# Seven half-width products for eight in the gate and up projections of two feed-forward layers

## The chip, the cores and the metric

The kernel runs on one core of a Trainium2 chip. The metric is the device time of one execution in microseconds (us), as the median of several runs.

## What is computed

Two transformer blocks run one after the other on one sequence of 512 tokens with a model width of 1024, in float32. The change touches their two feed-forward layers (D_FF is 2816):

```python
u = rms_norm(h, norm_ffn_g[l])
g, up = jnp.split(u @ w_gate_up[l], 2, axis=-1)
h = h + (jax.nn.silu(g) * up) @ w_down[l]
...
h = rmsnorm(x, g_ffn_pre[l])
gu = h @ w_ffn_in[l]
f = (jax.nn.silu(gu[..., :D_FF_2]) * gu[..., D_FF_2:]) @ w_ffn_out[l]
x = x + rmsnorm(f, g_ffn_post[l])
```

Around them stand attention, an mLSTM, gates and projections, which the change leaves as they are.

## The kernel before

**Data.** Activations are held transposed: 1024 features are 8 tiles of 128 partitions by 512 tokens (`hT`, float32). A float32 product is made of three matmuls in a rounded format, since each factor is split into a high part (the value rounded) and a low part (the rest): high times high, high times low, low times high (`split_mm`, L527 to L529). The normalised input is `u_hi` and `u_lo`, each 8 tiles; the products of gate and up are `a_hi` and `a_lo`, 22 tiles each (`FT` is 22).

**Weights.** All weights of the program are one stream of tiles of 128 x 1024 (512 KB), in the order of use. Tile t goes through a ring of three slots (`R` is 3). SyncE loads it into `w_raw` (the loop at L417) once the low part of tile t-3 is made. ScalarE rounds it into `w_hi` (`feed`, L1229, recorded at L1234) once TensorE has done with tile t-3 (semaphore `w_used`). GpSimd then makes `w_lo = w_raw - w_hi` (`low_part`, L440, recorded at L443), for nearly all tiles. TensorE waits for `lo_ready`.

**Up stages.** In `ffn1` and `ffn2` (44 tiles each) the tiles alternate: one of gate weights, one of up weights. Each is a unit of 24 matmuls of 512 columns into one PSUM bank (`tile_unit`, L531): 8 feature tiles by three. Six units, three pairs, are a turn of the loop (`tiles_loop`, L625). VectorE's part of a pair is `pair` in `ffn_dve` (L2335): the gate is scaled by the norm's factor (L2337), ScalarE takes its sigmoid (L1657), two multiplications of SBUF tiles follow (L2342, L2343), then the up product out of PSUM (L2345), and the high and low part of the result (L2348, L2349). The norm's factor comes late, so that it is multiplied in behind the matmuls (`root`, L1261; the matmul at L684 or L1139).

**Down stages.** `down` (L642) reads `a_hi` and `a_lo`. Its first unit waits until 20 of 22 tiles are split, its last for all of them.

Every engine has its own queue in program order. On VectorE, `step` lets each instruction wait until the one before it is done.

## Time and profile before

| | us |
|---|---|
| median of 3 runs (1701.81 to 1701.96) | 1701.86 |
| span of the profiled execution | 1699.9 |
| PE busy in that span | 1690.9 (99%) |
| DVE busy | 883.4 (52%) |
| ACT busy | 656.4 (39%) |
| POOL busy | 682.4 (40%) |

PE is TensorE, PEld its loading of stationary tiles, DVE VectorE, ACT ScalarE, POOL GpSimd, SP SyncE. The profiled execution's span is 2.0 us shorter than the median of the runs.
### The profile page before, as it was taken

Reading aid. Unit: us, or ns where it says so; the run is one execution under the profiler, and the core shown is the slowest. Engines: PE = TensorE matmul, PEld = TensorE weight load, DVE = VectorE, ACT = ScalarE, POOL = GpSimd, SP = SyncE. Lnnn points to the kernel's source line nnn. Section 1 sums busy time; section 2 is a strip of 40 time slices with the busy share of each in tenths; the row PEclk is TensorE's granted clock in tenths of the full one; section 3 lists DMA queues with packets and bytes.
Section 4 is the critical chain, followed back from the end, with each engine's and each line's share of the span. In section 5 each row is a group of like instructions: output and inputs, shape, how many; then the busy total and the mean of one; then the engine's idle time right before and its main releaser. Section 6 shows DMA issues by size and latency. Waiting matters only on the chain.

```text
span 1699.9 us, 23574 instructions
## 1 busy us (share of the span) xinstructions
PE 1690.9 (99%) x8081; PEld 1359.4 (80%) x8085; DVE 883.4 (52%) x1406; ACT 656.4 (39%) x1091; POOL 682.4 (40%) x308
## 2 busy tenths in 40 slices
PE   9999999999999999999999999999999999999998
PEld 7888767788888888888788766678888988888887
DVE  6644875564655551217497676642233775555013
ACT  7333544433222223327424576452223522222122
POOL 2444322344544444445343102544444344444443
PEclk9999999999999999999999999999999999999999
DMA  5345321223333223334322111122233232332332
GB/s 202 115 152 152 102 63 51 75 87 124 99 99 98 90 97 99 99 98 138 128 88 87 50 38 51 51 74 90 96 99 99 88 99 92 94 98 99 99 97 65
DMA packets 47635, 162.29 MB, mean 95 GB/s; under 512 B 5724, under 2 KB 7900, under 8 KB 47304
## 3 DMA queue, kind: packets, MB, share of 16 engines
q1 hardware_dynamic: 43440, 150.70, 28.1%
q10 hardware_dynamic: 4120, 10.59, 1.9%
q8 instruction: 46, 0.75, 0.2%
q14 instruction: 29, 0.24, 0.0%
HBM read 156.91 MB, written 4.76 MB: 95 GB/s over the span
## 4 chain that ended last, share of the span: by engine, by line
PE 52%; issue 32%; POOL 12%; ACT 1%; DVE 1%; DMA 1%; POOLq 0%; SPq 0%; ACTq 0%; DVEq 0%
PE ps L527 14%; PE ps L529 14%; PE ps L528 14%; POOL w_lo L443 12%; PE ps L1153 1%; PE ps L1152 1%; PE ps L1151 1%; PE ps L708 1%; PE ps L726 1%; PE ps L752 1%; PE ps L1052 1%; PE ps L1011 1%; PE ps L1033 1%; PE ps L980 1%; DMA hT<-xT 0%
## 5 line engine op out<-in xcount | busy, mean ns | idle before, releaser
L443 POOL TENSOR_TENSOR w_lo<-w_raw,w_hi 128x1024 fp32r<-128x1024 f32 x260 | 643.2, 2476 | 892.8 <-ACT w_hi L1234 866.1
L527 PE MATMUL ps<-u_hi,w_hi 128*128 128x512 f32 x1336 | 540.0, 404 | 0.2 <-ACTq L1824 0.2
L529 PE MATMUL ps<-u_hi,w_lo 128*128 128x512 f32 x1336 | 521.7, 390 | 0.0
L528 PE MATMUL ps<-u_lo,w_hi 128*128 128x512 f32 x1336 | 521.3, 390 | 0.0
L1234 ACT ACTIVATE w_hi<-w_raw 128x1024 fp32r<-128x1024 f32 x271 | 285.5, 1055 | 391.9 <-PE ps L529 326.4
L527 PEld LDWEIGHTS ps<-u_hi,w_hi 128*128 128x128 f32 x1336 | 251.2, 188 | 58.5 <-issue 8.6
L529 PEld LDWEIGHTS ps<-u_hi,w_lo 128*128 128x128 f32 x1336 | 250.9, 188 | 53.0
L528 PEld LDWEIGHTS ps<-u_lo,w_hi 128*128 128x128 f32 x1336 | 251.4, 188 | 51.1 <-issue 1.4
L1657 ACT ACTIVATE tmp<-tmp 128x512 f32<-128x512 f32 x44 | 27.8, 632 | 213.2 <-DVEq L2339 213.2
L2349 DVE TENSOR_TENSOR a_lo<-tmp,a_hi 128x512 f32 (+1 forms) x44 | 104.2, 2368 | 4.7
L527 PE MATMUL ps<-a_hi,w_hi 128*128 (+1 forms) x264 | 103.0, 390 | 0.0
L529 PE MATMUL ps<-a_hi,w_lo 128*128 (+1 forms) x264 | 102.8, 390 | 0.0
L528 PE MATMUL ps<-a_lo,w_hi 128*128 (+1 forms) x264 | 102.8, 390 | 0.0
L2345 DVE TENSOR_TENSOR tmp<-ps,tmp 128x512 f32<-128x512 f32 x44 | 30.4, 692 | 91.5 <-PE ps L529 91.2
L477 POOL TENSOR_TENSOR masked_bias<-bias,pick 128x128 f32<-128x128 f32 (+3 forms) x32 | 25.5, 824 | 104.5 <-PE ps L1052 103.7
L2337 DVE TENSOR_TENSOR tmp<-ps,tmp 128x512 f32<-128x512 f32 x44 | 30.4, 692 | 57.5 <-PE ps L529 43.9
L2306 DVE TENSOR_TENSOR tmp<-ps,tmp 128x512 f32<-128x512 f32 x16 | 11.1, 692 | 91.1 <-PE ps L529 90.0
L527 PEld LDWEIGHTS ps<-a_hi,w_hi 128*128 128x128 f32 x264 | 49.6, 188 | 10.4
L529 PEld LDWEIGHTS ps<-a_hi,w_lo 128*128 128x128 f32 x264 | 49.6, 188 | 10.3
L528 PEld LDWEIGHTS ps<-a_lo,w_hi 128*128 128x128 f32 x264 | 49.6, 188 | 10.1
L527 PE MATMUL ps<-m_hi,w_hi 128*128 128x512 f32 (+1 forms) x152 | 54.4, 358 | 0.0
L528 PE MATMUL ps<-m_lo,w_hi 128*128 128x512 f32 (+1 forms) x152 | 54.1, 356 | 0.0
(408 smaller groups left out, 2485.8 us busy)
## 6 DMA issues: line engine op xcount, KB each, us to landing
w_raw<-stream SPq DMA_DIRECT2D x277, 512.0 KB, 3.5
g_rep<-g_one ACTq DMA_DIRECT2D x1, 2560.0 KB, 13.7
spread<-m_rows ACTq DMA_DIRECT2D x4, 512.0 KB, 4.2
tmp<-tmp ACTq DMA_DIRECT2D x32, 64.0 KB, 2.7
bias<-g_rep ACTq DMA_DIRECT2D x1, 2048.0 KB, 9.7
outT<-hT SPq DMA_DIRECT2D x13, 128.0 KB, 2.0
hT<-xT SPq DMA_DIRECT2D x3, 512.0 KB, 7.0
mem_in<-memT ACTq DMA_DIRECT2D x1, 1024.0 KB, 4.7
```

Source lines behind the costliest of these rows:

```text
L443: pool.tensor_tensor(w_lo[:, slot], w_raw[:, slot], w_hi[:, slot].bitcast(F32), ALU.subtract)\
L477: pool.tensor_tensor(masked_bias[s % 4][:, 0:n], bias[:, h, T - n:T], pick[:, MOFF[t]:MOFF[t] + n], ALU.add).then_inc(named("dsa_bias"), 1)
L527: pe.matmul(out, wh, xh, start=start, stop=False)
L528: pe.matmul(out, wh, xl, start=False, stop=False)
L529: return pe.matmul(out, wl, xh, start=False, stop=stop)
L708: m = pe.matmul(ps[:, 2 + e, 0:keys[t]], head_q(h, t), head_k(h, keys[t]), start=True, stop=not extra(t))
L726: m = pe.matmul(ps[p0:p1, b, t * P:t * P + P], values(h, kb), prT[e][:, kb * P:kb * P + P], start=kb == 0, stop=kb == nb - 1)
L1234: act.activation(w_hi[:, slot], w_raw[:, slot], ACT.Copy).then_inc(hi_ready, 1)
L1657: act.activation(tmp[0][:, :], tmp[1][:, :], ACT.Sigmoid).then_inc(named(name + "_e"), 1)
L2337: step(dve.tensor_tensor(tmp[1][:, :], ps[:, banks[0], :], tmp[3][:, :], ALU.mult))
L2345: step(dve.tensor_tensor(tmp[4][:, :], ps[:, banks[1], :], tmp[2][:, :], ALU.mult))
L2349: step(dve.tensor_tensor(a_lo[:, bass.ds(k, 1)], a, a_hi[:, bass.ds(k, 1)].bitcast(F32), ALU.subtract))
```

## The change

Of every three pairs of the two up stages, two are computed by a scheme of Strassen's kind: a 2 x 2 product of blocks with seven block products in place of eight. The blocks are halves of the 1024 features, halves of the 512 tokens, and the gate and the up tile. A block product is 12 matmuls of 256 columns (`half_product`), a pair 84 of them, where it was 48 of 512 columns. The third pair stays as it was. `ffn1` has 6 such turns after 6 plain units, `ffn2` has 5 after 12, and 2 plain units close each stage.

Sums of weights are new (`weight_sums`, `s_raw`), and their split (`s_hi` on ScalarE, `s_lo` on VectorE in `sums_low`); sums of activations and their split (`t_sums`, `t_low`), four tiles once per stage; and sums of products out of PSUM (`copy` on ScalarE, `late_sums`, `late_up`, `fast_gate` on VectorE). The gate's sigmoid is written to PSUM bank 3 for these pairs, and `fast_up` multiplies there. The products of gate and up are kept as `a_raw` and split behind the last turn: the high part on ScalarE (`split`), the low part on VectorE. `down` waits for two more tiles before each of its units. SyncE waits for the weight sums before two of the six loads of a turn. The load of `mem_in` moves to the last turn of `ffn1`. `plain_gate`, `plain_mid` and `plain_up` hold the four multiplications of the old `pair` (one, two and one). Several semaphores are merged.

```diff
...
+                    for j in range(2 * R):
+                        t = u + R + j
+                        low, summed = i * (2 * R) + (t - R + 1), of_fast(name, "sum", i * 2 + (j // 2 + 1))
+                        if j in (0, 2):
+                            sp.wait_ge(*summed)
+                        sp.wait_ge(lo_ready, low)
+                        sp.dma_start(w_raw[:, t % R], stream[bass.ds(i * (2 * R) + t, 1)].rearrange("a p n -> (a p) n"))\
+                          .then_inc(landed[t % R], 16)
...
+            def half_product(out, w_h, w_l, x_h, x_l, start, stop):
+                for k in range(HK):
+                    pe.matmul(out, w_h(k), x_h(k), start=start and k == 0, stop=False, skip_group_check=True)
+                    pe.matmul(out, w_h(k), x_l(k), start=False, stop=False, skip_group_check=True)
+                    m = pe.matmul(out, w_l(k), x_h(k), start=False, stop=stop and k == HK - 1, skip_group_check=True)
+                return m
...
+                pe.wait_ge(lo_ready, t + 1)
+                acquire(x)
+                half_product(ps[:, x, L], *natural(a, 0), *of_u(0, L), True, False)
+                pe.wait_ge(*of_fast(name, "s_lo", i * 2 + (e + 1)))
+                half_product(ps[:, x, H], *summed(1), *of_t(2), False, True).then_inc(prod, 1)
+                acquire(y)
+                half_product(ps[:, y, L], *summed(0), *of_t(1), True, False)
+                pe.wait_ge(lo_ready, t + 2)
+                half_product(ps[:, y, H], *natural(b, 0), *of_t(0), False, True).then_inc(prod, 1)
+                pe.wait_ge(*of_fast(name, "copied", i * 2 + (e + 1)))
+                half_product(ps[:, x, L], *natural(a, 1), *of_u(1, L), False, True).then_inc(w_used, 1)
+                half_product(ps[:, x, H], *natural(b, 1), *of_t(3), False, True).then_inc(w_used, 1)
+                pe.wait_ge(*of_fast(name, "z", i * 2 + (e + 2)))
+                half_product(ps[:, y, H], *summed(2), *of_u(1, H), False, True).then_inc(named("fast_s_used"), 1)
...
+                    summed(i, pair)
+                    act.wait_ge(*of_fast(name, "s_used", i * 2 + (pair % 3 + 2 * (pair // 3) + 1)))
+                    act.activation(s_hi[pair % 3][:, :, :], s_raw[:, :, :], ACT.Copy).then_inc(named("raw_hi"), 1)
...
+                def copy(i, e):
+                    act.wait_ge(*of_fast(name, "prod", i * 4 + (2 * e + 1)))
+                    act.wait_ge(*of_fast(name, "z", i * 2 + (e + 1)))
+                    act.activation(first_two[:, :], ps[:, ffn2_banks(e)[0], :], ACT.Copy)\
...
+                def turn(i, last):
+                    feed_at(i, 2)
+                    copy(i, 0)
+                    sums_hi(i, 1)
+                    feed_at(i, 3)
+                    feed_at(i, 4)
+                    gate(ps[:, E_BANK, :])
+                    copy(i, 1)
+                    feed_at(i, 5)
+                    feed_at(i, 6)
+                    gate(ps[:, E_BANK, :])
...
+                        sums_hi(i, 3)
+                        feed_at(i, 7)
+                        plain_gate()
+                first(FIRST[name], plain_gate, t_tile, sums_hi)
...
+            def one_turn(u, gate, t_tile, sums_hi):
+                feed_after(u)
+                t_tile(0)
+                t_tile(1)
+                root("n_ffn", T)
+                feed_after(u + 1)
+                sigmoids()
+                gate()
+                feed_after(u + 2)
+                t_tile(2)
+                t_tile(3)
+                feed_after(u + 3)
+                gate()
+                feed_after(u + 4)
+                sums_hi(0, 0)
+                feed_after(u + 5)
+                gate()
...
+                    if k >= 2:
+                        dve.wait_ge(*of_fast(name, "t_hi", k - 1))
+                    t1, t2, t3, t4 = [t_raw[k % 2][:, n] for n in range(4)]
+                    step(dve.tensor_scalar(b11, hT[:, k, L], col, None, ALU.mult))
+                    step(dve.scalar_tensor_tensor(out=t1, in0=hT[:, k, H], scalar=col, in1=b11,
+                                                  op0=ALU.mult, op1=ALU.subtract))
+                    step(dve.scalar_tensor_tensor(out=t2, in0=hT[:, HK + k, H], scalar=late, in1=t1,
+                                                  op0=ALU.mult, op1=ALU.subtract))
+                    step(dve.tensor_tensor(t3, t2, b11, ALU.subtract))
+                    step(dve.scalar_tensor_tensor(out=t4, in0=hT[:, HK + k, L], scalar=late, in1=t2,
+                                                  op0=ALU.mult, op1=ALU.subtract))
+                    dve.sem_inc(named("fast_sum"), 1)
...
+                def t_low(k):
+                    dve.wait_ge(*of_fast(name, "t_hi", k + 1))
+                    step(dve.tensor_tensor(t_lo[:, k], t_raw[k % 2][:, :, :], t_hi[:, k].bitcast(F32), ALU.subtract))
+                    dve.sem_inc(named("raw_lo"), 1)
...
+                def weight_sums(i, pair):
+                    c = u + 2 * pair
+                    a, b = c % R, (c + 1) % R
+                    for t in (c, c + 1):
+                        dve.wait_ge(landed[t % R], i * 32 + (16 * (t // R) + 16))
+                    step(dve.tensor_tensor(s_raw[:, 1], w_raw[:, a, 0:T], w_raw[:, b, 0:T], ALU.subtract))
+                    step(dve.tensor_tensor(w_raw[:, b, 0:T], w_raw[:, b, 0:T], w_raw[:, b, T:2 * T], ALU.add))
+                    step(dve.tensor_tensor(s_raw[:, 0], w_raw[:, b, 0:T], w_raw[:, a, 0:T], ALU.subtract))
+                    step(dve.tensor_tensor(s_raw[:, 2], w_raw[:, a, T:2 * T], s_raw[:, 0], ALU.subtract))
+                    dve.sem_inc(named("fast_sum"), 1)
+                def sums_low(i, pair):
+                    dve.wait_ge(*of_fast(name, "s_hi", i * 2 + (pair % 3 + 2 * (pair // 3) + 1)))
+                    step(dve.tensor_tensor(s_lo[pair % 3][:, :, :], s_raw[:, :, :], s_hi[pair % 3][:, :, :].bitcast(F32),
+                                           ALU.subtract))
...
+                def late_sums(i, e):
+                    dve.wait_ge(*of_fast(name, "prod", i * 4 + (2 * e + 2)))
+                    dve.wait_ge(*of_fast(name, "copied", i * 2 + (e + 1)))
+                    step(dve.tensor_tensor(late_two[:, :], ps[:, ffn2_banks(e)[1], :], first_two[:, :], ALU.add))
+                    dve.sem_inc(named("fast_z"), 1)
+                def late_up():
+                    step(dve.tensor_tensor(late_two[:, H], late_two[:, H], late_two[:, L], ALU.add))
+                def fast_gate(i, e):
+                    x, y = ffn2_banks(e)
+                    dve.wait_ge(*of_fast(name, "s_used", i * 2 + (e + 3)))
+                    step(dve.tensor_tensor(tmp[1][:, H], ps[:, y, H], late_two[:, L], ALU.add))
+                    dve.sem_inc(bank_free[y], 1)
+                    step(dve.tensor_tensor(tmp[1][:, L], ps[:, x, L], rs[:, L], ALU.mult))
+                    step(dve.tensor_tensor(tmp[1][:, H], tmp[1][:, H], rs[:, H], ALU.mult))
+                    dve.sem_inc(named("fast_gate"), 1)
+                    step(dve.tensor_tensor(late_two[:, L], ps[:, x, H], late_two[:, L], ALU.add))
+                    dve.sem_inc(bank_free[x], 1)
+                def fast_up(k):
+                    made.use()
+                    dve.wait_ge(*of_fast(name, "e", made.value()))
+                    x = ps[:, E_BANK, :]
+                    step(dve.tensor_tensor(x, x, tmp[1][:, :], ALU.mult))
+                    step(dve.tensor_tensor(x, x, rs[:, :], ALU.mult))
+                    step(dve.tensor_tensor(a_raw[:, bass.ds(k, 1)], x.unsqueeze(1), late_two[:, :].unsqueeze(1), ALU.mult))
+                    dve.sem_inc(named("fast_a"), 1)
...
+                def turn(i, last):
+                    k = (u - f) // 2
+                    plain_up(i * (2 * R) + (u - 1), ffn2_banks(2)[1], i * R + (k - 1))
+                    weight_sums(i, 1)
+                    late_sums(i, 0)
+                    sums_low(i, 1)
+                    late_up()
+                    fast_gate(i, 0)
+                    fast_up(i * R + k)
+                    late_sums(i, 1)
+                    late_up()
+                    fast_gate(i, 1)
+                    if not last:
+                        weight_sums(i, 3)
+                    fast_up(i * R + (k + 1))
+                    plain_gate(i * (2 * R) + (u + 4), ffn2_banks(2)[0])
+                    if not last:
+                        sums_low(i, 3)
+                    plain_mid()
...
+                if name == "ffn1":
+                    two_t_tiles(0)
+                    dve.wait_ge(*of_norm("n_" + gain, "rs", 1))
+                    pair(0, ffn_banks(0))
+                    two_t_tiles(2)
+                    pair(1, ffn_banks(1))
+                else:
...
+                    pair(4, ffn2_banks(1))
+                weight_sums(0, 0)
+                plain_gate(u - 2, ffn2_banks(2)[0])
+                sums_low(0, 0)
...
```

## Rows read from the trace of the kernel before

**Rows 1.** The page, its busy times, and its granted clock and slices.
```profile
span 1699.9 us, 23574 instructions
PE 1690.9 (99%) x8081; PEld 1359.4 (80%) x8085; DVE 883.4 (52%) x1406; ACT 656.4 (39%) x1091; POOL 682.4 (40%) x308
PEclk9999999999999999999999999999999999999999
```

**Rows 2.** The longest of TensorE's waits: us in total, times, longest.
```profile
PE ps L820 <- DVE blank L2060: 1.2, 1, 1.2
PE ps L1052 <- issue: 0.6, 4, 0.2
```

**Rows 3.** Busy time by stretch, inside the loops of ffn1 and ffn2.
```profile
core 0: us, PE busy (x) PEld busy (x) DVE busy (x) ACT busy (x) POOL busy (x), PEclk, DMA share, GB/s
437.00:644.00 207.00, 207.00 (x915) 171.53 (x914) 111.92 (x115) 51.52 (x58) 99.52 (x39) 1.00 0.31 96
1410.00:1573.00 163.00, 163.00 (x721) 135.07 (x720) 88.01 (x91) 40.95 (x46) 77.09 (x30) 1.00 0.31 97
```

**Rows 4.** TensorE in order of time: start, duration; 24 matmuls of 512 columns.
```profile
519.87 0.39 PE L527 MATMUL ps<-u_hi,w_hi 128*128 128x512 f32 x1
...
525.31 0.39 PE L527 MATMUL ps<-u_hi,w_hi 128*128 128x512 f32 x1
```

**Rows 5.** The same in the last stage: 24 matmuls of 256 columns, then 48.
```profile
1672.65 0.28 PE L1151 MATMUL ps<-a_hi,w_hi 128*128 128x256 f32 x1
...
1675.52 0.28 PE L1151 MATMUL ps<-a_hi,w_hi 128*128 128x256 f32 x1
...
1681.28 0.28 PE L1151 MATMUL ps<-a_hi,w_hi 128*128 128x256 f32 x1
```

**Rows 6.** VectorE in order of time, ffn1's loop and its first pairs.
```profile
426.68 0.69 DVE L2343 TENSOR_TENSOR tmp<-tmp,tmp 128x512 f32<-128x512 f32 x1
427.41 0.69 DVE L2345 TENSOR_TENSOR tmp<-ps,tmp 128x512 f32<-128x512 f32 x1
428.25 1.67 DVE L2348 TENSOR_SCALAR a_hi<-tmp 128x512 fp32r<-128x512 f32 x1
429.96 2.76 DVE L2349 TENSOR_TENSOR a_lo<-tmp,a_hi 128x512 fp32r<-128x512 f32 x1
...
504.00 2.68 DVE L2349 TENSOR_TENSOR a_lo<-tmp,a_hi 128x512 f32 x1
```

**Rows 7.** GpSimd in order of time, the same stretches.
```profile
426.95 5.22 POOL L443 TENSOR_TENSOR w_lo<-w_raw,w_hi 128x1024 fp32r<-128x1024 f32 x2 [5.27 <-ACT w_hi L1234]
...
503.52 2.60 POOL L443 TENSOR_TENSOR w_lo<-w_raw,w_hi 128x1024 fp32r<-128x1024 f32 x1 [1.37 <-ACT w_hi L1234]
```

**Rows 8.** VectorE and GpSimd in order of time, in an earlier stage.
```profile
360.60 1.53 DVE L2277 TENSOR_TENSOR tmp<-ps,g1a 128x512 f32<-128x512 f32 x2 [0.22 <-DVE tmp L2277]
362.27 1.79 DVE L2282 TENSOR_TENSOR tmp<-tmp,tmp 128x512 f32<-128x512 f32 x1
...
361.11 2.40 POOL L443 TENSOR_TENSOR w_lo<-w_raw,w_hi 128x1024 fp32r<-128x1024 f32 x1 [3.04 <-ACT w_hi L1234]
```

**Rows 9.** Groups by shape, whole span: busy us, mean ns.
```profile
L2460 DVE TENSOR_TENSOR w_lo<-w_raw,w_hi 128x1024 fp32r<-128x1024 f32 x8 | 9.7, 1215 | 0.0
L1979 DVE TENSOR_TENSOR um_lo<-tmp,um_hi 128x256 fp32r<-128x256 f32 x8 | 3.4, 421 | 0.2
L2543 DVE TENSOR_TENSOR hT<-ps,hT 128x256 f32<-128x256 f32 x16 | 6.7, 419 | 0.0
L1234 ACT ACTIVATE w_hi<-w_raw 128x1024 fp32r<-128x1024 f32 x271 | 285.5, 1055 | 391.9 <-PE ps L529 326.4 <-PE ps L1153 33.5 <-issue 20.4
L1657 ACT ACTIVATE tmp<-tmp 128x512 f32<-128x512 f32 x44 | 27.8, 632 | 213.2 <-DVEq L2339 213.2
```

**Rows 10.** The start of ffn1 in order of time: TensorE, VectorE, ScalarE.
```profile
403.36 0.39 PE L527 MATMUL ps<-u_hi,w_hi 128*128 128x512 f32 x1
...
406.43 0.69 DVE L1967 TENSOR_TENSOR tmp<-tmp,tmp 128x512 f32<-128x512 f32 x1
415.41 0.69 DVE L2337 TENSOR_TENSOR tmp<-ps,tmp 128x512 f32<-128x512 f32 x1 [8.29 <-ACT tmp L1265]
...
414.75 0.63 ACT L1265 ACTIVATE tmp<-tmp 128x512 f32<-128x512 f32 x1
```

**Rows 11.** DMA issues: KB each, median us from issue to landing.
```profile
w_raw<-stream SPq DMA_DIRECT2D x277, 512.0 KB, 3.5
```

More of the change, by code:

```diff
@@ new lines, in pair, with t_sums @@
+                def pair(j, banks):
+                    plain_gate(f + 2 * j, banks[0])
+                    plain_mid()
+                    plain_up(f + 2 * j + 1, banks[1], j)
+                def t_sums(k):
+                    col, late = v(gain, k), v(gain, HK + k)
+                    b11 = late_two[:, L]
+                    if k >= 2:
[10 more added lines that the diff above has]
+                    dve.sem_inc(named("fast_sum"), 1)
```

313 lines of the change are left out of this document (217 added, 96 removed).

## The prediction

> **What bounds the kernel now.** I read the page first: TensorE is busy for 99% of the span the others for 52% or less [rows 1]. Its granted clock is 1.00, the 2.4 GHz level, in both stretches that change [rows 3]. Then the waits of TensorE: the longest in total is 1.2 us, at the start [rows 2]. So each column that TensorE is spared counts in full, as long as the others keep up. Third, the busy time by stretch inside the two loops that change: in 207 us of ffn1, VectorE 111.9 us, ScalarE 51.5 us, GpSimd 99.5 us [rows 3]. VectorE looks half idle. The reader should keep in mind that this is before the change puts most of its new work there, and that VectorE and GpSimd hold each other up, which is the point on which this prediction turns.
>
> **What TensorE is spared.** Twenty-four matmuls of 512 columns take 525.31 - 519.87 = 5.44 us, 0.2267 us each [rows 4]. A pair is 48 of them, 10.88 us, a turn of three pairs 32.64 us. Twenty-four matmuls of 256 columns take 2.87 us, and 72 take 8.63 us, 0.1198 us each [rows 5]. A pair by seven products is 84 of these, 10.06 us; a half-width product takes 1.44 us. A turn is then 2 x 10.06 + 10.88 = 31.0 us, 1.64 us less, and 11 turns (6 and 5) save 18.0 us. Loading the stationary tiles twice as often per column is already in the 0.1198. The Trainium skill ("TensorE: Matmul & The Clock Gate", Back-to-back issue gap) gives N/2.4 + 2.5 ns for an isolated matmul, 109 ns for 256 columns; by that and its 216 ns for 512 an estimate of the saving would be 26 us. The rows disagree, and the sum goes by the rows.
>
> **How VectorE and GpSimd hold each other up.** VectorE's subtraction of two SBUF tiles of 512 columns takes 0.69 us alone, but 2.68 us when it starts at 504.00, inside GpSimd's 503.52 to 506.12: it ends 0.56 us behind GpSimd's end [rows 6, 7]. So the later one waits for all of the other's instruction. With one operand in PSUM there is no such wait: two of them take 1.53 us across GpSimd's start at 361.11, and the next, of two SBUF tiles, ends only 0.55 us behind GpSimd's end at 363.51 [rows 8]. When GpSimd has two tiles in line (426.95, 5.22 us), a blocked VectorE instruction gets in between them (it ends at 429.92), and the one behind it waits for the second (to 432.72) [rows 6, 7]. So they take turns. The Trainium skill says the same ("SBUF — State Buffer", Who interferes with whom): a VectorE instruction with two SBUF inputs contends with a GpSimd instruction that reads SBUF, and the second one blocks fully. That is the rule that speaks against this change, and the trace agrees.
>
> **VectorE's own work in a turn after.** One after the other, dependent instructions of 512 columns start 0.73 us apart [rows 6], of 1024 take 1.215 us, of 256 0.42 us [rows 9]; 1536 columns are then 1.215 + (1.215 - 0.69) = 1.74 us, 1.78 with the step between. Counted from the diff, a turn has:
> - with a PSUM operand, 512 columns: plain_up, plain_gate, two late_sums, six in fast_up: 10 x 0.73 = 7.3 us
> - of two SBUF tiles, 512 columns: eight in weight_sums, two in plain_mid: 7.3 us
> - sums_low: 2 x 1.78 = 3.6 us
> - 256 columns: six with PSUM in fast_gate, and four of SBUF tiles alone (late_up and fast_gate's third): 10 x 0.46 = 4.6 us.
>
> That is 22.8 us. Each semaphore increment behind a step costs some 0.11 us (a gap of 0.15 us ahead of L2348, against 0.04 us without) [rows 6]; 18 in a turn are 2.0 us, of which I let half fall into waits, and the moving address of a_raw adds 0.3 us. Own work: 24.1 us, well under 31.0.
>
> **What is added by GpSimd.** It still makes six low parts in a turn, each 2.4 us [rows 8]. I laid one turn out from the durations above, in the order of the queues, with ScalarE at 1.06 us for a tile, 0.63 us for a sigmoid or copy and 1.06 + 0.42 = 1.48 us for the sums' high part (0.42 is the step from 512 to 1024 columns) [rows 9]. The steady turn, in us from its first product: VectorE ends sums_low(3) of the turn before at 2.4. Plain_mid stands behind GpSimd (2.4 to 4.8) and ends at 6.0, plain_up 6.9, weight_sums 9.9, late_sums 10.7; ScalarE's high part is there at 11.5, sums_low ends 13.3; late_up, behind GpSimd (13.3 to 15.7), 16.1; fast_gate's third instruction, behind GpSimd (16.1 to 18.5), 19.0, its fourth 19.5; the sigmoid is there at 19.8, fast_up ends 22.3, late_sums 23.0, late_up 23.5; the seventh product of the second pair ends at 24.8, fast_gate 26.7; weight_sums, behind GpSimd (26.3 to 28.7), 31.5; fast_up 33.9, plain_gate 34.7; sums_low, behind GpSimd (34.1 to 36.5), 38.1. That is 35.7 behind the 2.4 of the start. On TensorE the second product starts at 2.4, the fifth of the second pair at 20.5 behind ScalarE's copy, the plain units run from 24.8 to 35.7. So GpSimd costs VectorE 2.4 us on plain_mid, 2.4 on late_up, 1.5 on fast_gate, 1.9 on weight_sums and 1.5 on the second sums_low; its fourth low part lies in a wait for TensorE. Together 9.7 us. Waits for ScalarE's high part of the sums (0.8), for a sigmoid (0.3) and for the seventh product (1.2) make 2.3 us. VectorE's turn: 24.1 + 9.7 + 2.3 = 36.1 us (the layout's 35.7 is without increments and the moving address, of which part is covered), taken as **36.2 us against 32.64 us before**. Even a turn that starts with VectorE on time comes out some 5 us behind TensorE's 31.0 us, so it can't be caught up. TensorE would then wait at three places of a turn: for s_lo ahead of the second product (about 1.5 to 2.4 us, because sums_low(3) stands behind GpSimd), for late_sums ahead of the seventh (about 1), and for ScalarE's copy ahead of the fifth product of the second pair (about 2.5), since that copy is queued behind the sigmoid, which waits for fast_gate.
>
> **The ends of the stages.** In ffn1 the 6 plain units have t_sums and t_low for four tiles beside them: about 2.2 us of sums (five of 256 columns) and 1.25 us of low part a tile, 14 us, of which the first half fits into the 8.3 us in which VectorE waits for the norm's factor [rows 10]. The rest delays the feed of the sixth tile (queued on ScalarE behind t_tile(3)) by about 1.7 us, and the first weight sums by 2.3 us beyond the steady place: 4.0 us. In ffn2, with 12 plain units, it fits; its first turn begins on time and costs 32.4 us by the layout. Behind the last turn 22 high parts (0.63) and low parts (0.73, some behind GpSimd) run beside four plain units (21.8 us) and the down stage, which takes two tiles in 5.44 us: at no cost, hidden behind those units. SyncE's new waits cost nothing: the load of a pair's second tile is issued about 3 us before its slot is wanted by the slowed VectorE or earlier, landing takes 3.5 us [rows 11], and if that cover were gone weight_sums would start 1 us late. The mem_in load is hidden by the down stage.
>
> **The sum**, on the profiled span: 4.0 + 6 x 3.56 = 25.4 us in ffn1; (32.4 - 32.64) + 4 x 3.56 = 14.0 us in ffn2; together +39.4 us. 1699.9 + 39.4 = 1739.3 us span; the median stands 2.0 us over the span, so **1741 us**. For the bounds, a VectorE turn of 34.8 us (all increments hidden, blocks of 8.5 us) gives +25 and one of 38 us (every low part falling on it) +57: 1727 to 1760 us.
>
> **Rivals.**
> - **TensorE stays the bound** (faster). If the low parts fall mostly beside VectorE's 10.1 us of PSUM work and its idle time, blocks of 4 to 5 us fit. For it: two-SBUF work (12.7 us) and GpSimd (14.4 us) together are 27 us, under 31.0. Against it: GpSimd starts right after ScalarE's feed, which is released by TensorE, and the layout puts five of six on such work. Then -18.0 + 4.0 (start of ffn1) = 1688 us; with 0 to 1 us of waits a turn, 1688 to 1699.
> - **In between**: a turn of 33 to 34.8 us. 4 + 11 x 0.4 = +8 at one end, +27 at the other: about 1706 to 1728, some of it near no change when the start is cheaper.
> - **TensorE and VectorE in lockstep** (slower still): each of TensorE's three waits moves w_used, so feeds, low parts and blocks follow later and VectorE waits again for the seventh product. It decides if VectorE's waits for TensorE pass 4 us a turn: 39 us a turn gives 1772 us.
> - **The seven products don't pay**: if 256 columns cost over 10.88 / 84 = 0.1295 us, nothing is saved. The rows show 0.1198 over 72 in a row, with the same loads [rows 5]; a wait of 0.05 us between products would leave 0.5 of 0.82 us a pair. It moves the second rival, not the forecast.
>
> **How the numbers follow.** VectorE-bound as forecast 0.55; slower still 0.05; in between 0.16; TensorE-bound 0.24. A measurement here can tell 0.2% (3.4 us) from no change. Faster: 0.24 and a little of the in-between, 0.25; within 0.2%: 0.05; slower: 0.70. The range takes in both sides, 1687 to 1763 us, and leaves out under 0.2; the likeliest case alone has 1727 to 1760.
>
> **What would show it.** In the profile after: matmuls of 256 columns 0.12 us apart within a product; PE busy well under 99% of a longer span, with gaps ahead of the second, seventh and, in the second pair, fifth product, released by DVE s_lo, DVE late_two and ACT first_two; a turn of 36 us; weight_sums, plain_mid, late_up and sums_low with means well over their 0.69, 0.69, 0.42 and 1.74 us; VectorE's busy share in the turns over 90%. Wrong would be: a turn of 31 us, means near the bare durations, or waits of TensorE named after DMA or GpSimd's w_lo.

## The result, and the profile after

| | before | after |
|---|---|---|
| median | 1701.91 us (1701.81 to 1702.22) | 1771.86 us (1771.69 to 1771.90) |
| ratio | | 1.0409, 95% interval 1.0394 to 1.0424 |
| span of the profiled execution | 1699.9 us | 1770.1 us |

The change makes the kernel 4.1% slower. The forecast was slower, 1741 us with a range of 1687 to 1763: the sign was right, and the time lies 31 us above the forecast and 9 us above the range.

The page of the kernel after, its busy times and its granted clock, against [rows 1]:

```profile
span 1770.1 us, 25791 instructions
PE 1698.0 (96%) x8873; PEld 1397.2 (79%) x8877; DVE 1083.9 (61%) x1630; ACT 730.5 (41%) x1187; POOL 693.4 (39%) x308
PEclk9999999999999998999999999999999989999999
```

TensorE's count of matmuls rises by 792 (two of every three pairs have 84 of half the width for 48), and it is now idle for 72 us. Its busy time rises by 7.1 us, although the scheme spares it 18.0 by the forecast: a part of its matmuls runs at the lower clock, as shown below. VectorE is busy for 200 us more. The waits of TensorE, against [rows 2], where the longest total was 1.2 us (engine, line waited for, releaser: us in total, times, longest):

```profile
PE ps L585 <- POOL w_lo L501: 20.8, 3, 9.7
PE ps L703 <- DVEq L2607: 17.4, 10, 2.0
PE ps L703 <- DVEq L2614: 15.0, 11, 2.0
PE ps L703 <- ACT tmp L1782: 9.7, 8, 1.2
```

L703 is the first matmul of a half-width product. Its three rows are the waits inside the turns: for `s_lo` ahead of the second product (the increment at L2607), for `late_two` ahead of the seventh (L2614), for ScalarE's copy `first_two` ahead of the fifth (L1782). The first row is something else: three waits for GpSimd's `w_lo` at ordinary units, 20.8 us in all, and they lie outside the turns.

Where each stretch ends (the first matmul of the next, from TensorE's rows in order of time), and what it adds:

| stretch | ends, before | ends, after | adds | forecast |
|---|---|---|---|---|
| all ahead of ffn1 | 403.36 | 403.97 | 0.6 | 0 |
| ffn1's 6 plain units | 436.91 | 442.09 | 4.6 | 4.0 |
| its 6 turns and 2 plain units | 643.63 | 673.23 | 24.4 | 21.4 |
| down1a and all up to ffn2's fourth tile | 1345.32 | 1387.28 | 12.4 | 0 |
| ffn2's plain units | 1395.21 | 1448.68 | 11.5 | 0 |
| its 5 turns and 2 plain units | 1569.29 | 1639.52 | 16.8 | 14.0 |
| sum | | | 70.2 | 39.4 |

Two stretches forecast at nothing carry 24 of the 31 us that the forecast was short.

**Inside a turn.** TensorE in order of time: a turn starts at 517.07 and the next at 553.58, 36.5 us later (before: 32.64 [rows 4]). In between stand the waits, and behind the first of them, in this turn, the clock falls:

```profile
517.07 0.28 PE L703 MATMUL ps<-u_hi,w_hi 128*128 128x256 f32 x1
...
520.41 0.38 PE L703 MATMUL ps<-t_hi,s_hi 128*128 128x256 f32 x1 [1.75 <-DVEq L2607]
...
521.76 0.41 PE L703 MATMUL ps<-t_hi,s_hi 128*128 128x256 f32 x1
521.97 0.41 PE L704 MATMUL ps<-t_lo,s_hi 128*128 128x256 f32 x1
...
553.58 0.28 PE L703 MATMUL ps<-u_hi,w_hi 128*128 128x256 f32 x1
```

VectorE and GpSimd in the same turn. A duration of 2.4 us for 256 columns, or 2.97 for 1536, is an instruction held up (bare 0.42 [rows 9] and 1.76, as the same L2605 shows at 530.12):

```profile
517.33 2.97 DVE L2605 TENSOR_TENSOR s_lo<-s_raw,s_hi 128x1536 fp32r<-128x1536 f32 x1 [0.31 <-DVE tmp L2535]
520.52 2.56 DVE L2543 TENSOR_TENSOR tmp<-tmp,tmp 128x512 f32<-128x512 f32 x1 [0.22 <-DVE s_lo L2605]
...
530.12 1.76 DVE L2605 TENSOR_TENSOR s_lo<-s_raw,s_hi 128x1536 fp32r<-128x1536 f32 x1 [0.67 <-ACT s_hi L1776]
532.02 2.40 DVE L2618 TENSOR_TENSOR tmp<-tmp 128x256 f32<-128x256 f32 x1
...
535.57 1.38 DVE L2627 TENSOR_TENSOR tmp<-tmp,tmp 128x256 f32<-128x256 f32 x1
...
541.17 2.60 DVE L2618 TENSOR_TENSOR tmp<-tmp 128x256 f32<-128x256 f32 x1
...
544.93 1.38 DVE L2627 TENSOR_TENSOR tmp<-tmp,tmp 128x256 f32<-128x256 f32 x1
```
```profile
516.28 2.40 POOL L501 TENSOR_TENSOR w_lo<-w_raw,w_hi 128x1024 fp32r<-128x1024 f32 x1 [6.70 <-ACT w_hi L1358]
518.86 3.67 POOL L501 TENSOR_TENSOR w_lo<-w_raw,w_hi 128x1024 fp32r<-128x1024 f32 x1 [0.18 <-ACT w_hi L1358]
531.11 5.57 POOL L501 TENSOR_TENSOR w_lo<-w_raw,w_hi 128x1024 fp32r<-128x1024 f32 x2 [8.58 <-ACT w_hi L1358]
541.08 4.94 POOL L501 TENSOR_TENSOR w_lo<-w_raw,w_hi 128x1024 fp32r<-128x1024 f32 x2 [4.41 <-ACT w_hi L1358]
```

Over the bare durations VectorE spends 1.2 us on `s_lo`, 1.9 on `plain_mid`, 2.0 and 2.2 on `late_up`, 1.0 and 1.0 on `fast_gate`'s third operation: 9.2 us held up (forecast 9.7). The weight sums were free of it, and the second `late_up` was hit in their place. The only waits in VectorE's turn beyond the steps from one instruction to the next are 0.7 us for ScalarE's high part and 0.2 for a sigmoid: VectorE sets the turn, and in it TensorE's product is not what it waits for. (It waits for one only in the last turn of each stage, 1.6 us.)

**At the ends.** Ahead of down1a's second tile, VectorE, ScalarE, GpSimd and TensorE in order of time:

```profile
677.31 9.92 DVE L2646 TENSOR_TENSOR a_lo<-a_raw,a_hi 128x512 fp32r<-128x512 f32 x12 [0.25 <-DVE a_raw L2549]
687.45 3.60 DVE L2160 TENSOR_TENSOR tmp<-tmp,tmp 128x256 f32<-128x256 f32 x7 [0.22 <-DVE a_lo L2646]
```
```profile
679.73 0.73 ACT L1383 ACTIVATE tmp<-mem_in 128x256 f32<-128x256 f32 x2
687.91 2.53 ACT L1383 ACTIVATE tmp<-mem_in 128x256 f32<-128x256 f32 x5 [7.45 <-DVE tmp L2160]
690.35 1.99 ACT L1358 ACTIVATE w_hi<-w_raw 128x1024 fp32r<-128x1024 f32 x2
```
```profile
691.47 2.36 POOL L501 TENSOR_TENSOR w_lo<-w_raw,w_hi 128x1024 fp32r<-128x1024 f32 x1 [19.77 <-ACT w_hi L1358]
```
```profile
693.97 0.79 PE L585 MATMUL ps<-a_hi,w_hi 128*128 x1 [9.71 <-POOL w_lo L501]
694.56 0.63 PE L586 MATMUL ps<-a_lo,w_hi 128*128 x1
694.99 0.63 PE L587 MATMUL ps<-a_hi,w_lo 128*128 x1
```

Read it from the end: TensorE waits 9.7 us for `w_lo`, GpSimd for ScalarE's `w_hi`, which is queued behind the squares of the memory's norm; five of these wait for VectorE's adds of them; and these stand behind VectorE's 12 `a_lo` splits, which the change put there. No wait of TensorE is named after the splits: they are early enough for `down`. What isn't is the work queued behind them.

Ahead of ffn2's first turn, ScalarE, VectorE and TensorE in order of time:

```profile
1428.32 1.06 ACT L1761 ACTIVATE t_hi<-t_raw 128x1024 fp32r<-128x1024 f32 x1 [1.84 <-DVEq L2575]
1431.99 0.63 ACT L1753 ACTIVATE tmp<-tmp 128x512 f32<-128x512 f32 x1 [2.61 <-DVEq L2537]
1435.91 0.63 ACT L1753 ACTIVATE tmp<-tmp 128x512 f32<-128x512 f32 x1 [3.30 <-DVEq L2537]
1436.45 1.99 ACT L1358 ACTIVATE w_hi<-w_raw 128x1024 fp32r<-128x1024 f32 x2
```
```profile
1439.04 1.71 DVE L2596 TENSOR_TENSOR s_raw<-w_raw 128x512 f32<-128x512 f32 x1 [0.32 <-DVE a_raw L2549]
1440.78 2.74 DVE L2597 TENSOR_TENSOR w_raw<-w_raw 128x512 f32<-128x512 f32 x1
...
1446.58 1.76 DVE L2605 TENSOR_TENSOR s_lo<-s_raw,s_hi 128x1536 fp32r<-128x1536 f32 x1 [0.77 <-ACT s_hi L1776]
```
```profile
1440.26 0.79 PE L585 MATMUL ps<-u_hi,w_hi 128*128 128x512 f32 x1 [8.36 <-POOL w_lo L501]
```

Here the feeds stand behind two sigmoids, and these behind VectorE, which is late with its pairs because of the activation sums; and even without the feeds, the `s_lo` of the first turn is there only at 1448.3. From the norm's factor (its first use is at 1398.0) that is 50.3 us of VectorE's queue. TensorE's plain units, 49.9 us from 1387.28 on as before, and the first product leave it until 1438.6, 40.6 us. Of the 9.7 us that are missing, about 8.0 are operations held up by GpSimd, each against its bare duration: 1.9, 2.0 and 1.1 us in the activation sums, 1.0 and 2.1 in the weight sums above.

### The profile page after: what moved, and what is told of

It reads as the page before. It is cut to its first block, busy times and chain, and to the rows that moved or that the text cites. A ratio compares the mean times of both kernels' runs of the same rounds, so it can differ in the third digit from the quotient of the medians.

```text
span 1770.1 us, 25791 instructions
## 1 busy us (share of the span) xinstructions
PE 1698.0 (96%) x8873; PEld 1397.2 (79%) x8877; DVE 1083.9 (61%) x1630; ACT 730.5 (41%) x1187; POOL 693.4 (39%) x308
## 4 chain that ended last, share of the span: by engine, by line
PE 45%; issue 29%; DVE 12%; POOL 10%; ACT 2%; DMA 1%; DVEq 0%; POOLq 0%; SPq 0%; ACTq 0%
PE ps L585 12%; PE ps L586 12%; PE ps L587 12%; POOL w_lo L501 10%; DVE s_lo L2605 1%; DVE tmp L2618 1%; PE ps L1277 1%; PE ps L1275 1%; PE ps L1276 1%; PE ps L825 1%; PE ps L843 1%; DVE tmp L2543 1%; DVE tmp L2627 1%; PE ps L869 1%; PE ps L1173 1%
## 5 line engine op out<-in xcount | busy, mean ns | idle before, releaser
L585 PE MATMUL ps<-u_hi,w_hi 128*128 128x512 f32 x984 | 404.6, 411 | 11.3 <-POOL w_lo L501 11.1
L587 PE MATMUL ps<-u_hi,w_lo 128*128 128x512 f32 x984 | 385.8, 392 | 0.0
L586 PE MATMUL ps<-u_lo,w_hi 128*128 128x512 f32 x984 | 385.7, 392 | 0.0
L585 PEld LDWEIGHTS ps<-u_hi,w_hi 128*128 128x128 f32 x984 | 186.0, 189 | 57.1 <-POOL w_lo L501 12.2
L587 PEld LDWEIGHTS ps<-u_hi,w_lo 128*128 128x128 f32 x984 | 185.8, 189 | 40.2
L586 PEld LDWEIGHTS ps<-u_lo,w_hi 128*128 128x128 f32 x984 | 186.3, 189 | 37.2 <-issue 1.4
L703 PE MATMUL ps<-t_hi,s_hi 128*128 128x256 f32 x176 | 52.9, 300 | 17.4 <-DVEq L2607 17.4
L2499 DVE TENSOR_TENSOR tmp<-ps,tmp 128x512 f32<-128x512 f32 x16 | 11.1, 691 | 91.1 <-PE ps L587 90.0
L703 PE MATMUL ps<-u_hi,w_hi 128*128 128x256 f32 x176 | 51.6, 293 | 9.7 <-ACT tmp L1782 9.7
L2605 DVE TENSOR_TENSOR s_lo<-s_raw,s_hi 128x1536 fp32r<-128x1536 f32 x22 | 49.6, 2255 | 11.7 <-ACT s_hi L1776 8.9
L587 PE MATMUL ps<-m_hi,w_lo 128*128 128x512 f32 (+1 forms) x152 | 54.1, 356 | 0.0
```

The source lines that it names most:

```text
L585: pe.matmul(out, wh, xh, start=start, stop=False)
L586: pe.matmul(out, wh, xl, start=False, stop=False)
L587: return pe.matmul(out, wl, xh, start=False, stop=stop)
L703: pe.matmul(out, w_h(k), x_h(k), start=start and k == 0, stop=False, skip_group_check=True)
L2605: step(dve.tensor_tensor(s_lo[pair % 3][:, :, :], s_raw[:, :, :], s_hi[pair % 3][:, :, :].bitcast(F32), ALU.subtract))
```

## The experiments

All are timed against the kernel before on the same chip, whose median there was 1702.2 to 1702.6 us, and the ratios are to that. "Less" means less than the changed kernel's 1771.9 us, which was timed beside a kernel before of 1701.9, so that differences under a microsecond or two say nothing. The theory is that of the prediction with its ends mended: VectorE, held up by GpSimd, sets the turns (41 us), and what the change puts on VectorE ahead of and behind the turns holds up ScalarE's feeds (24 us). The rivals are named with each run.

**The feeds ahead of the squares.** Down1a's first three feeds move ahead of the squares that wait for VectorE.

```diff
...
+            u = FIRST["down1a"]
+            feed_after(u)
             for k in range(KT):
                 square("n_mem", lambda k: mem_in[:, k], MEM, k)
+                if k == 2:
+                    feed_after(u + 1)
+                    feed_after(u + 2)
-            down_act("down1a", "n_fin", lambda k: hT[:, k], 0, memory_split)
+            down_act("down1a", "n_fin", lambda k: hT[:, k], 0, memory_split, fed=3)
...
```

> The changed kernel with one reordering on ScalarE at the end of ffn1: the feeds of the tiles two to four places ahead no longer stand behind the eight squares of the memory norm, whose last five wait for VectorE's additions, which stand behind its 22 low parts. Theory 1 (the queue order on ScalarE makes TensorE's wait of 9.7 us in down1a, and the slow clock behind it costs another 2.2 us): 1771.9 - 11.9 = 1760 us. Rival (TensorE would wait there anyway, for a_lo, which VectorE makes until 687 us): the wait only changes its name, and the time stays over 1768 us.

Measured: 1760.00 us (ratio 1.0339, 1.0322 to 1.0356), 11.9 us less, what theory 1 said. The 9.7 us wait is gone; 11.1 us in two waits for `w_lo` are left. So this stretch of the accounting is the order of ScalarE's queue behind VectorE's splits, with the slow clock that follows the wait.

**ffn2's feeds early.** The feeds of tiles 11 and 12 move ahead of the activation copies and the sigmoids.

```diff
                 gate()
                 feed_after(u + 8)
+                feed_after(u + 9)
                 t_tile(2)
                 t_tile(3)
+                feed_after(u + 10)
                 gate()
                 gate()
-                feed_after(u + 9)
-                feed_after(u + 10)
```

> The changed kernel with the feeds of ffn2's twelfth and thirteenth tile moved ahead of the activation sums' high parts and of two sigmoids on ScalarE. Theory 1 (TensorE's wait of 8.4 us ahead of the twelfth tile is made by ScalarE's order): about 11 us less with the slow clock behind it, 1761 us. Theory 2 (VectorE is behind with its whole work ahead of the first turn, and s_lo of the first pair is not there before some 1448 us in the trace): the wait moves to the second product of the first turn and keeps its length; 1770 us or more, at most 2 us gained.

Measured: 1770.97 us (ratio 1.0402, 1.0385 to 1.0419), no different from the changed kernel: theory 2. TensorE's longest wait between 1430 and 1470 us shows where the 8.4 us went:

```profile
PE ps L703 <- DVEq L2607: 9.1, 1, 9.1
```

The wait for `w_lo` has become one for `s_lo`. The releaser that the profile named was only the first of two late ones; the cause is VectorE's backlog.

**ScalarE's copy ahead of the sigmoid.** In each turn the copy for the second pair goes ahead of the sigmoid of the first.

```diff
...
+                    copy(i, 1)
                     gate(ps[:, E_BANK, :])
-                    copy(i, 1)
...
```

> The changed kernel with ScalarE's copy of the second pair's first two products ahead of the first pair's sigmoid. Theory 1 (a turn is as long as VectorE's queue; in it VectorE waits some 1.2 us for the seventh product, which is late because of this copy): a turn of 36.5 us becomes about 35.3 us, 11 turns give -13 us, 1759 us. Rival (the low parts on GpSimd move with w_used, and what VectorE saves in waiting it loses in being blocked): within 3 us of 1772 us.

Measured: 1761.25 us (1.0344, 1.0326 to 1.0361), 10.6 us less. The wait for `first_two` vanishes, the one for `late_two` grows from 15.0 to 28.6 us in all, the one for `s_lo` falls from 17.4 to 5.5. So the third of the predicted waits was real, and about 1 us a turn could be had by order alone. The number is near theory 1's, its reason isn't what the traces show: in the changed kernel VectorE doesn't wait for the seventh product in a steady turn, so there was no such wait to save. A steady turn is now 34.98 us (517.13 to 552.11), 1.5 less. VectorE's second `late_up` in it, and what follows:

```profile
539.70 1.11 DVE L2618 TENSOR_TENSOR tmp<-tmp 128x256 f32<-128x256 f32 x1
541.40 0.42 DVE L2624 TENSOR_TENSOR tmp<-ps,tmp 128x256 f32<-128x256 f32 x1 [0.60 <-PE ps L705]
```

`late_up` took 2.60 us before and takes 1.11, `fast_gate`'s third 1.38 and now 0.92, and a wait of 0.6 us for the product is new. GpSimd's low parts moved with the copy (they start at 538.15, ahead of `late_sums`), so that less of them falls on VectorE: 2.0 us less hold-up for 0.6 of waiting. That the gain came out near the 13 us of theory 1 is luck.

**GpSimd's low part in two halves.** The same work in two operations of 512 columns, so that VectorE gets in between.

```diff
...
-                pool.tensor_tensor(w_lo[:, slot], w_raw[:, slot], w_hi[:, slot].bitcast(F32), ALU.subtract)\
-                    .then_inc(lo_ready, 1)
+                for c in (slice(0, T), slice(T, DM)):
+                    m = pool.tensor_tensor(w_lo[:, slot, c], w_raw[:, slot, c], w_hi[:, slot, c].bitcast(F32),
+                                           ALU.subtract)
+                m.then_inc(lo_ready, 1)
...
```

> The changed kernel with GpSimd's low part of nearly every tile made by two instructions of 512 columns in place of one of 1024. Theory 1 (VectorE waits for the whole of a GpSimd instruction, and the two take turns): a single blocked instruction (late_up, the third of fast_gate, sums_low) waits 1.2 us in place of 2.4, the pair in plain_mid and the four in weight_sums lose the same; about 3 us a turn, 11 turns give -33 us, 1739 us. Rival (what counts is GpSimd's time in all, some 15 us a turn, however it is cut): 1772 us or, with the second instruction's fixed time, a little over.

Measured: 1733.14 us (1.0182, 1.0165 to 1.0199), 38.7 us less from an edit of a few lines: theory 1, and some 6 us more than it said. A turn is 33.47 us (530.39 to 563.86). Two of the operations above, `late_up` and `plain_mid`'s first, in a turn of this kernel:

```profile
528.88 1.49 DVE L2620 TENSOR_TENSOR tmp<-tmp 128x256 f32<-128x256 f32 x1
...
542.75 1.49 DVE L2545 TENSOR_TENSOR tmp<-tmp,tmp 128x512 f32<-128x512 f32 x1 [0.22 <-DVE s_lo L2607]
```

`late_up` takes 1.5 us in place of 2.4, `plain_mid` 1.5 in place of 2.6. GpSimd itself pays: 766 us busy in place of 693, off the path.

**Products in PSUM.** GpSimd is left alone; the held-up operations of the turns get an operand in PSUM (two free banks), at the price of one more operation of 256 columns for each late sum. `plain_mid`'s two products go through `mid` in the same way.

```diff
...
+                late_ps = ps[:, 2, :]
+                mid = ps[:, E_BANK, :]
...
-                    step(dve.tensor_tensor(late_two[:, :], ps[:, ffn2_banks(e)[1], :], first_two[:, :], ALU.add))
+                    y = ffn2_banks(e)[1]
+                    step(dve.tensor_tensor(late_two[:, L], ps[:, y, L], first_two[:, L], ALU.add))
+                    step(dve.tensor_tensor(late_ps[:, H], ps[:, y, H], first_two[:, H], ALU.add))
...
-                    step(dve.tensor_tensor(late_two[:, H], late_two[:, H], late_two[:, L], ALU.add))
+                    step(dve.tensor_tensor(late_two[:, H], late_ps[:, H], late_two[:, L], ALU.add))
...
-                    step(dve.tensor_tensor(tmp[1][:, H], ps[:, y, H], late_two[:, L], ALU.add))
+                    step(dve.tensor_tensor(mid[:, H], ps[:, y, H], late_two[:, L], ALU.add))
...
-                    step(dve.tensor_tensor(tmp[1][:, H], tmp[1][:, H], rs[:, H], ALU.mult))
+                    step(dve.tensor_tensor(tmp[1][:, H], mid[:, H], rs[:, H], ALU.mult))
...
```

> Edit: in the turns, VectorE's late sum of the right half, fast_gate's first sum and plain_mid's first product are written to free PSUM banks, so that late_up, fast_gate's third operation and both of plain_mid's have one PSUM operand, as the operations that the trace shows not held up by GpSimd; the late sum becomes two operations of 256 columns. Everything is computed. Theory 1 (it is the held-up SBUF-only operations on the chain that lengthen the turn: per turn late_up 2 x 1.9 us, plain_mid 1.6, fast_gate 2 x 1.0, together 7.4, against 5.0 us of TensorE waits per turn): these waits mostly go, turn about 32.5 to 33.5 us, 1733 us (1722 to 1745). Theory 2 (GpSimd's 9.7 us per turn only move to the SBUF-only operations that are left, weight_sums and s_lo): turn 35 us or more, at least 1756 us. The waits at the stage ends stay in both.

Measured: 1731.05 us (1.0165, 1.0148 to 1.0182), 40.8 us less, theory 1; a turn is 31.86 us (502.63 to 534.49). VectorE's groups between 450 and 600 us, `late_up`, `fast_gate`'s third, `plain_mid`'s first, and what is still held up:

```profile
L2626 DVE TENSOR_TENSOR tmp<-ps,tmp 128x256 f32<-128x256 f32 x10 | 4.2, 424 | 1.5
L2635 DVE TENSOR_TENSOR tmp<-ps,tmp 128x256 f32<-128x256 f32 x10 | 4.2, 424 | 0.3
L2546 DVE TENSOR_TENSOR ps<-ps,tmp 128x512 f32<-128x512 f32 x4 | 2.8, 700 | 0.9 <-DVE s_lo L2611 0.9
L2611 DVE TENSOR_TENSOR s_lo<-s_raw,s_hi 128x1536 fp32r<-128x1536 f32 x9 | 20.6, 2291 | 3.7 <-ACT s_hi L1776 2.5 <-DVE tmp L2537 1.2
L2602 DVE TENSOR_TENSOR s_raw<-w_raw 128x512 f32<-128x512 f32 x9 | 8.4, 934 | 3.2 <-DVE a_raw L2555 2.0 <-DVE tmp L2637 1.2
```

Each operation that got its PSUM operand takes its bare time, though GpSimd does the same work. What GpSimd still holds up in these turns is `s_lo` (0.5 us on average) and the first weight sum (0.24); the hold-up didn't move to them in full, as theory 2 had it.

**The gains together.** Halves, both orders, without and then with the products in PSUM.

> Edit: the low part in halves, the copy ahead of the gate, and the feeds ahead of the squares, without the products in PSUM. Everything is computed. Theory 1 (gains at different places add, but the halves have already taken the wait for ScalarE's copy down from 1.2 to 0.25 us, so its order is worth nothing more): 1733.1 - 11.9 = 1721 us (1718 to 1724). Theory 2 (all three add in full, 38.7 + 11.9 + 10.6): 1711 us.

Measured: 1717.22 us (1.0088, 1.0071 to 1.0104): 3.8 us below theory 1 and just under its range, 6 above theory 2. If the feeds' order again gave its 11.9 us, the copy's is worth 4 us behind the halves, where it gave 10.6 alone; no run has these two apart.

> Edit: products in PSUM, GpSimd's low part in two halves, ScalarE's copy ahead of the gate, and down1a's first feeds ahead of the squares, together. Everything is computed. Theory 1 (with the halves the turn was 33.47 us with 1.6 + 0.25 us of waits; both go and the turn is TensorE's own 31.6 to 31.9; down1a gives 12 us back): 1733.1 - 11 x 1.7 - 12 = 1702 us (1698 to 1708), no different from the kernel before. Theory 2 (the additional half-width operation of each late sum puts back what is won): 1715 us or more.

Measured: 1702.85 us (1.0003, 0.9993 to 1.0012), as fast as the kernel before, as theory 1 said. A turn is 31.15 us (525.44 to 556.59), and beyond the first turns TensorE waits no more in the loops. Left are 8.6 us at ffn2's start and, in and ahead of the first turns, 1.6, 2.4, 0.8 and 1.2.

**Without GpSimd's low part in the turns.** This takes the hold-up out of the turns. It also has each `w_lo` ready some 2 us sooner, but no wait in the turns was named after it.

> Left out: of GpSimd's low part of each weight tile all but 32 of 1024 columns, in the turns of both stages alone. This separates VectorE's own work from the time in which GpSimd holds it up. Theory 1 (without GpSimd's operation VectorE has some 26 us of work in a turn, and TensorE sets the turn with its own 31.0 to 31.6 us): 1771.9 - 11 x 5.1 = 1716 us (1710 to 1722), the waits at the stage ends as they were. Theory 2 (VectorE's own chain or ScalarE's order hold the turn anyway): turn 33 us or more, at least 1735 us.

Measured: 1712.61 us (1.0059, 1.0042 to 1.0075), 59.3 us less: theory 1. A turn in this kernel, 524.55 to 555.61, by busy time, and VectorE's longest waits in it:

```profile
524.55:555.61 31.06, 31.06 (x218) 29.17 (x217) 21.63 (x32) 12.14 (x13) 2.40 (x7) 1.00 0.32 101
```
```profile
DVE tmp L2631 <- PE ps L712: 3.0, 1, 3.0
DVE tmp L2620 <- PE ps L712: 1.2, 1, 1.2
DVE s_lo L2612 <- ACT s_hi L1783: 0.7, 1, 0.7
```

TensorE is busy all 31.06 us, VectorE waits 4.2 us for it and 0.9 for ScalarE, so that VectorE's own work is 31.06 - 5.1 = 26.0 us. The turn of the changed kernel is 26.0 + 9.2 + 0.9 = 36.1 us by these terms, 36.5 measured; a wait has the ordinary step of some 0.1 us between two instructions in it, and four of them make most of the 0.4. In a turn of TensorE's length VectorE had 4.2 us of room, and the hold-up of 9.2 is what makes it the bound.

**ffn2's start.** Two reorderings: the activation sums ahead of the norm's result, first on top of all the others, then alone in the changed kernel; and the sums laid into the gaps in which VectorE waits for the sigmoid.

```diff
...
+                    t_sums(0)
+                    t_sums(1)
                     dve.wait_ge(*of_norm("n_" + gain, "rs", 1))
                     pair(0, ffn2_banks(0))
                     pair(1, ffn2_banks(1))
-                    two_t_tiles(0)
+                    t_low(0)
+                    t_low(1)
+                    two_t_tiles(2)
                     pair(2, ffn2_banks(2))
-                    two_t_tiles(2)
                     pair(3, ffn2_banks(0))
...
```

> Edit: on top of the version with products in PSUM, halves and both orders, VectorE makes the first two activation sums of ffn2 in the 4.4 us in which it is idle ahead of the norm's result (1348.6 to 1353.0), and the other two ahead of the third pair, and ScalarE's feeds of tiles 11 and 12 of the stage move ahead of a gate accordingly. Everything is computed. Theory 1 (TensorE's 8.6 us wait at 1386.9 is VectorE's backlog, and it fits once the sums lie in idle time): 1702.9 - 8.6 - 1.2 (a wait for late_two in the first turn that goes with it) = 1693 us (1690 to 1696), faster than the kernel before. Theory 2 (the wait moves to the second product, which waits for s_lo, as with the feeds alone): 1699 to 1703 us.

Measured: 1699.11 us, 11 runs (ratio 0.9979, 0.9970 to 0.9988): inside theory 2's range, at its lower end, and a little faster than the kernel before. The 8.6 us wait shrank to 2.4, and 2.3 us for `s_lo` stand behind it. `s_lo` of the first turn ends at 1399.0 where it ended at 1402.8, and the time fell by the same 3.7 us. It fell no further because `t_sums(0)` is itself held up by GpSimd (four operations of 1.4 us in place of 0.4 to 0.5), and ScalarE's root, queued behind its high part, comes 4.5 us later.

> Edit: the same reordering of ffn2's activation sums and of the gates beside them, made in the changed kernel alone. Everything is computed. Theory 1 (VectorE's order ahead of the first fast turn of ffn2 costs the 8.4 us wait and the slow clock behind it, 11.5 us together; with GpSimd's whole-width low parts some of it stays): 1771.9 - 8 to 11 = 1762 us (1760 to 1765). Theory 2 (wait moves to the second product): 1768 us or more.

Measured: 1768.62 us (1.0389, 1.0373 to 1.0404), 3.2 us less: theory 2's number, a miss for theory 1. Of the 8.4 us, 3.3 stay at `w_lo`, 0.8 appear at `s_lo`, and the wait for `late_two` in the first turn grows from 1.9 to 3.5: with whole-width low parts VectorE hasn't the time in this order either.

> Edit: on top of the version with products in PSUM, halves and both orders, the activation sums and low parts lie in the gaps of 0.85 to 1.7 us in which VectorE waits for ScalarE's gate, in both stages (one in VectorE's idle time ahead of ffn2's norm result, ffn2's first weight sums in the fifth pair's gap), with ScalarE's feeds between its copies accordingly; nothing is put ahead of ScalarE's root. Everything is computed. Theory 1 (the first turn of each stage starts when VectorE's work ahead of s_lo is done, and every gap that is filled brings it forward by its length: ffn2 some 8 us earlier than in that version, ffn1 some 3 us): 1702.9 - 8 - 3 = 1692 us (1689 to 1696). Theory 2 (the reordering only moves the wait to GpSimd's low part of the weights, as VectorE's work now collides with it): 1698 us or more.

Measured: 1698.51 us (0.9975, 0.9965 to 0.9985), no different from the other order: theory 2. GpSimd now falls on the activation sums (ffn1's `t_sums(2)`, 416.66 to 422.65, 6.0 us in place of 2.3), and TensorE waits 4.4 us for `s_lo` there, where it waited 2.4.

**No hold-up in the stages at all.** The last kernel, with GpSimd's low parts cut in the plain units of both stages too.

> Left out, on top of the version with the sums in the gates' gaps (without the halves): of GpSimd's low part of each weight tile all but 32 of 1024 columns, from the first tile of both up stages to the end of their turns, so that VectorE is held up nowhere in them. Theory 1 (the 9.8 us that TensorE still waits around the first turns, 4.4 + 1.3 + 2.3 + 1.0 + 0.8, come from VectorE being held up in the prologues): 1698.5 - 8 to 10 = 1690 us (1688 to 1692). Theory 2 (VectorE's own work in the prologues is too much for the 35 to 55 us that TensorE leaves it): 1695 us or more.

Measured: 1685.34 us (0.9901, 0.9885 to 0.9918), below both. TensorE's longest waits in the whole kernel; those in the two stages are gone:

```profile
PE ps L943 <- DVE blank L2266: 1.2, 1, 1.2
PE ps L807 <- DVE tmp L2173: 0.9, 2, 0.6
```

The theory had counted only the waits that were left; the clock that falls behind them comes back too (mean 1.000 in place of 0.997). Of the waits counted, 1.8 us were for `w_lo` itself, which this edit also makes sooner, so that not all of the gain is VectorE's. This kernel isn't a version to use, since it leaves work out. It shows what the seven products are worth where nothing stands in their way: 1702.3 - 1685.3 = 17.0 us.

## Why the prediction was right or wrong

- **TensorE's saving: right.** 31.0 us a turn was forecast, 31.06 is measured once VectorE keeps up; 18.0 us in all was forecast, 17.0 measured without hold-up.
- **How VectorE and GpSimd hold each other up: right** where it was used: in full for two SBUF operands, not at all with one in PSUM (`late_up`: 424 ns in place of some 2500), in turns where GpSimd has two in line. It was too narrow in one point: an operation of one SBUF tile can be held up too, as the 1.67 us of L2348 in [rows 6] already show. The whole-width low part is what makes it dear: halves gave 38.7 us, no low part 59.3.
- **VectorE's turn: right in sum, by two errors that cancel.** Own work 24.1 forecast, 26.0 measured; waits 2.3 forecast, 0.9 measured; hold-up 9.7 forecast, 9.2 measured. Together 36.2 against 36.5 in the steady turns of both stages. About 1.0 of the 1.9 us by which the own work was short is the half of the increments that the prediction let "fall into waits": there were hardly any waits for them to fall into. The rest lies in gaps between instructions, as the 0.67 us ahead of `plain_up`, where 0.3 was allowed. The places of the hold-up differ as well (both `late_up`, no weight sum); that their sum came out is in part luck.
- **TensorE's three waits: right** in place and releaser. In size, 1.7, 1.7 and 1.2 us in a steady turn, the first was right (1.5 to 2.4), the second larger than forecast (1), the third half of it (2.5). No engine in the turns waits for a DMA, as forecast of SyncE's waits.
- **ffn1's start: right,** 4.6 us for 4.0.
- **The first turns: too small.** ffn1's first lasts 38.5 us where 36.2 were counted, ffn2's 34.7 where 32.4 were. In both, `plain_mid` is held up on both of its operations; in ffn1:

```profile
445.70 2.63 DVE L2543 TENSOR_TENSOR tmp<-tmp,tmp 128x512 f32<-128x512 f32 x1
448.37 2.75 DVE L2544 TENSOR_TENSOR tmp<-tmp,tmp 128x512 f32<-128x512 f32 x1
```

That is 4.0 us, where a steady turn loses 1.9 there, and most of the 3.0 and 2.8 us by which the two stages' turns are over.
- **"At no cost, hidden behind those units": wrong, and 12.4 us.** This is the first step that failed. The prediction asked whether the splits come in time for `down`. They do. It didn't ask what else is queued behind them on VectorE and ScalarE. The wait is named after GpSimd's `w_lo`, which the prediction had listed as a sign of being wrong. The memory norm's squares and adds go through both engines in turn, and the feeds of `down` stand behind them. Moving the feeds ahead gave 11.9 us back.
- **ffn2's start, "with 12 plain units, it fits": wrong, and 11.5 us.** The second step that failed. It counted units and not VectorE's time. Between the norm's factor and the first `s_lo` VectorE has 5 pairs (with about 0.85 us for each sigmoid), four tiles of sums, weight sums and 8.0 us of hold-ups, 50.3 us where TensorE leaves it 40.6. In ffn1 the same work was laid against 6 units and costed; in ffn2 it wasn't laid out at all.
- **The range was too narrow** for the same reason: its bounds came from the turn alone, 34.8 to 38 us, and nothing in it stood for the ends of the stages. The rival at 1772 us would have given the right number by the wrong way: it has a turn of 39 us, and VectorE waiting for TensorE's seventh product for over 4 us a turn, where it waits 1.6 us in two of the 11 turns.

## What to carry to other kernels

Before work is moved onto an engine that looks half idle, count what it shares with another engine at the same time: here 9.2 us a turn of hold-up, where VectorE's 26.0 us of own work and 0.9 of waits left 4.2 in a turn of 31.06, to win 1.6. An operand in PSUM or a GpSimd operation in halves takes a large part of it away. When work is put off to the end of a stage, ask of every engine's queue what stands behind it and who waits for that, and not only whether the work itself is in time. When a wait's releaser is mended and the wait moves (from `w_lo` to `s_lo`, 8.4 to 9.1 us), the engine behind both is the cause.
